# A state space recurrence taken two time steps at a time, inside a two-block transformer kernel

## What is computed

```python
lr, li = f32(lam_re), f32(lam_im)
dt = jnp.exp(f32(log_dt))[:, None]
mag = jnp.exp(lr * dt)
ar, ai = mag * jnp.cos(li * dt), mag * jnp.sin(li * dt)      # lambda
...
bbar_re = kr[..., None] * br - ki[..., None] * bi            # B
bbar_im = kr[..., None] * bi + ki[..., None] * br
def step(carry, uc):                                         # x[t] = lambda x[t-1] + B u[t]
    bur = jnp.einsum('lbgh,gph->lbgp', uc, bbar_re)
    bui = jnp.einsum('lbgh,gph->lbgp', uc, bbar_im)
    _, _, sr, si = lax.associative_scan(_complex_affine_combine, (a_r, a_i, bur, bui), axis=0)
    ...
    y = jnp.einsum('ghp,lbgp->lbgh', cr, xr) - jnp.einsum('ghp,lbgp->lbgh', ci, xi)
y = y + f32(d_skip) * f32(u)
g = jax.nn.gelu(y)
val, gate = jnp.split(g @ w_glu + b_glu, 2, axis=-1)
return val * jax.nn.sigmoid(gate)
```

## Time and profile before

| | us |
|---|---|
| median of 3 runs (lowest, highest) | 2593.39 (2592.49, 2596.54) |
| profiled execution | 2592.58 |
| its span, first to last instruction | 2590.5 |
| PE busy | 2421.6 (93%) |
| DVE busy | 1809.1 (70%) |
| ACT busy | 1261.3 (49%) |
| POOL busy | 159.4 (6%) |
| chain that ended last: PE, DVE, ACT | 84%, 10%, 3% of the span |

### The profile page before, as it was taken

The page is one execution under the profiler, slowest core; times in us unless marked ns, Lnnn a source line. Parts: engine busy times, 40 slices in busy tenths (PEclk is TensorE's granted clock), DMA queues, the critical chain, the costliest instruction groups (busy, mean ns, idle before and its releaser), DMA issues.

```text
span 2590.5 us, 31848 instructions
## 1 busy us (share of the span) xinstructions
PE 2421.6 (93%) x12441; PEld 1937.3 (75%) x12441; DVE 1809.1 (70%) x1966; ACT 1261.3 (49%) x1290; POOL 159.4 (6%) x142
## 2 busy tenths in 40 slices
PE   7999999999999999989989965689999999999996
PEld 6878858788878678789658852367888887887885
DVE  5763348857852477685545459968888888898887
ACT  3432334334322434344334444537667677776674
POOL 0000000000000000000100006500000000000000
PEclk9999999999999999999999985789999999999998
DMA  9767158657756287543245530138999989998994
...
DMA packets 303413, 586.14 MB, mean 226 GB/s; under 512 B 61439, under 2 KB 96965, under 8 KB 303181
## 3 DMA queue, kind: packets, MB, share of 16 engines
...
HBM read 583.60 MB, written 1.06 MB: 226 GB/s over the span
## 4 chain that ended last, share of the span: by engine, by line
PE 84%; DVE 10%; ACT 3%; issue 2%; DMA 1%; DVEq 0%; SPq 0%; ACTq 0%
PE psum L862 19%; PE psum L864 19%; PE psum L863 19%; PE psum L1326 3%; PE psum L895 3%; PE psum L1333 2%; PE psum L1388 2%; PE psum L2049 2%; PE psum L985 2%; DVE ring_r L1062 2%; PE psum L2673 2%; PE psum L2828 1%; PE psum L2851 1%; ACT ring_r L1056 1%; PE psum L1946 1%
## 5 line engine op out<-in xcount | busy, mean ns | idle before, releaser
L1062 DVE TENSOR_TENSOR ring_r<-ring,ring_r 128x2048 fp32r<-128x2048 f32 x286 | 652.6, 2289 | 291.4 <-ACT ring_r L1056 291.0
L1056 ACT CAST ring_r<-ring 128x2048 fp32r<-128x2048 f32 x286 | 545.2, 1910 | 507.3 <-PE psum L864 412.8
L864 PE MATMUL psum<-ring_r,arena_r 128*128 128x512 f32 (+1 forms) x1560 | 596.9, 383 | 0.0
L862 PE MATMUL psum<-ring_r,arena_r 128*128 128x512 f32 (+1 forms) x1016 | 400.3, 394 | 10.1 <-DVE arena_r L2846 5.2
L1062 DVE TENSOR_TENSOR ring_r<-ring,tail_r 128x2048 fp32r<-128x2048 f32 x143 | 327.2, 2288 | 95.9 <-ACT tail_r L1056 95.8
L863 PE MATMUL psum<-ring_r,arena_r 128*128 128x512 f32 (+1 forms) x1016 | 390.6, 384 | 0.0
L1056 ACT CAST tail_r<-ring 128x2048 fp32r<-128x2048 f32 x143 | 273.2, 1910 | 145.3 <-PE psum L864 139.3
L864 PEld LDWEIGHTS psum<-ring_r,arena_r 128*128 128x128 f32 x1560 | 294.4, 189 | 58.4
L864 PE MATMUL psum<-ring_r,z_r 128*128 128x512 f32 (+1 forms) x840 | 310.6, 370 | 0.0
L862 PEld LDWEIGHTS psum<-ring_r,arena_r 128*128 128x128 f32 x1016 | 192.3, 189 | 57.9 <-issue 18.5
L863 PEld LDWEIGHTS psum<-ring_r,arena_r 128*128 128x128 f32 x1016 | 192.3, 189 | 37.7 <-issue 1.9
...
## 6 DMA issues: line engine op xcount, KB each, us to landing
...
```

Of the source, the lines that this page charges most:

```text
L862: pe.matmul(dst, lhs_low, rhs, start=start, stop=False)
L864: return pe.matmul(dst, lhs, rhs_low, start=False, stop=stop)
L1056: act.copy(upper[i % UPPERS], place(PN[r.key, i])).then_inc(upper_ready, 1)
L1062: dve.tensor_tensor(low, raw, upper[i % UPPERS], ALU.subtract).then_inc(lower_ready, 1)
```

## The change

Time is split into 128 pairs of steps. The state is kept only at even steps: x[2m] = lambda^2 x[2m-2] + lambda B u[2m-1] + B u[2m], so B gets a second copy, `b_next` = lambda B, the drive of a pair is the sum of two matmuls, and scans have 128 steps with factor mag^2 (`l_mag2`). The even outputs are C x[2m]; the odd ones are (C lambda) x[2m] + K u[2m+1], where K = C B is a matrix of one block (`same_step` on PE, 32x32 tiles; `copy_kernel` on ACT). C lambda (`CT_next`) is made on POOL. The rotation is needed at 128 steps only. All buffers of the stage halve, so `scanned` has eight places instead of four.

Moved: the scaling of B goes from behind feed-forward 4 into four of its last iterations (pieces 0 to 3, two for B and two for lambda B); the loads of C are issued at the end of feed-forward 4 and not after the last turning of B; the turnings of lambda B lie on PE in units 0 and 2; outputs of block k come in step 2k+4, and the last but one behind the loop; GELU of the first half and the first three weight roundings lie on ACT behind the last placing of C. The skip term of block k is added two blocks later.

```diff
@@ -1162,6 +1180,8 @@
+            if r.n == 4 and "s5" in stages and UP_HALVES + 4 <= i < UP_HALVES + 8:
+                s5_scale_b_dve(dve, step, i - UP_HALVES - 4)
...
@@ -2297,28 +2317,36 @@
+    PAIRS = SEQ // 2
...
+    rot = cv.take(2, 2, QUAD, PAIRS)
+    glu_xh = Carve(cv.at, of=arena_r).take(KD, SEQ)
...
+        act.activation(l_mag2, lam_dt, ACT.Exp, scale=2.0).then_inc(*s5A.inc("mag2"))
...
+        for out_, other, op in ((l_kr2, l_ki, ALU.subtract), (l_ki2, l_kr, ALU.add)):
+            dve.tensor_tensor(l_t1, l_lr, l_kr if out_ is l_kr2 else l_ki, ALU.mult)
+            link(dve.tensor_tensor(l_t2, l_sin, other, ALU.mult))
+            link(dve.tensor_tensor(out_, l_t1, l_t2, op))
...
-        sp.wait_ge(*s5P.after("bt3"))
+        sp.wait_ge(halves_used, 5 * FFN_HALVES)
...
+            if k >= 2 and n % 2 == 0:
-            pool.tensor_tensor(prods[k % 2][:, 0:2, j, :], scanned[:, n % 4, :, :, :], both(r[:, 0, :, :]), ALU.mult)
-            pool.tensor_tensor(prods[k % 2][:, 2:4, j, :], scanned[:, n % 4, :, :, :], both(r[:, 1, :, :]), ALU.mult)\
-                .then_inc(*s5G.inc(f"x{n}"))
+            pool.tensor_tensor(prods[:, k % 2, 0:2, j, :], scanned[:, n % 8], both(r[:, 0]), ALU.mult)
+            pool.tensor_tensor(prods[:, k % 2, 2:4, j, :], scanned[:, n % 8], both(r[:, 1]), ALU.mult).then_inc(*s5G.inc(f"x{n}"))
+            if n % 2 == 0:
+                continue
+            c, after = CT[:, k % 2], CT_next[:, k % 2]
+            pool.wait_ge(*s5A.after(f"ct{k}"))
+            if k >= 1:
+                pool.wait_ge(*s5G.after(f"c{k - 1}"))
+            pool.tensor_tensor(after, c, lam_of(l_lr, k, 3), ALU.mult)
+            pool.tensor_tensor(c_part, c[:, 0:2], lam_of(l_sin, k, 2), ALU.mult).then_inc(*step.one())
+            pool.wait_ge(*step.now())
+            pool.tensor_tensor(after[:, 0], after[:, 0], c_part[:, 1], ALU.add)
+            pool.tensor_tensor(after[:, 1], after[:, 1], c_part[:, 0], ALU.subtract)
+            pool.tensor_tensor(after[:, 2], after[:, 2], c_part[:, 1], ALU.subtract).then_inc(*s5G.inc(f"c{k}"))
...
+        def copy_kernel(k):
+
+            act.wait_ge(*s5P.after(f"kb{k}"))
+            act.copy(kernel_0[:, k % 2, :], bank(7)[:, SEQ:SEQ + P]).then_inc(*s5A.inc(f"kc{k}"))
...
         angles(0)
         rotations(0)
+        copy_b(4)
+        copy_b(5)
         for k in range(KD):
             if k + 1 < KD:
                 angles(k + 1)
             place_c(k)
+            if k >= 1:
+                copy_kernel(k - 1)
             if k + 1 < KD:
                 rotations(k + 1)
+            else:
+                gelu(act, 0)
+            if k == 0:
+                copy_b(6)
+                copy_b(7)
+        copy_kernel(KD - 1)
         act.copy(glu_ones, ones[0:1, :]).then_inc(*s5A.inc("ones"))
         act.wait_ge(bias_landed, 16)
         act.copy(bias_hi, z_row[0:1, :]).then_inc(*s5A.inc("bias"))
-        gelu(act, 0)
         glu_upper_act(act, 0, None)
-        glu_upper_act(act, 1, s5V.after(f"in{S5_UNITS - 1}"))
+        glu_upper_act(act, 1, None)
+        glu_upper_act(act, 2, None)
         gelu(act, 1)
-        glu_upper_act(act, 2, s5P.after("y7"))
-        glu_upper_act(act, 3, None)
...
-                mag = l_mag[:, state:state + 1].to_broadcast([P, SEQ])
+                mag = l_mag2[:, state:state + 1].to_broadcast([P, PAIRS])
                 for i in range(2):
-                    ins = dve.tensor_tensor_scan(scanned[:, n % 4, i, jj, :], mag, bu[:, 1 - i, jj, :], 0.0, ALU.mult, ALU.add)
+                    ins = dve.tensor_tensor_scan(scanned[:, n % 8, i, jj, :], mag, bu[:, 1 - i, jj, :], 0.0, ALU.mult, ALU.add)
             ins.then_inc(*s5V.inc(f"scan{n}"))
-            if n % 2 and k >= 1:
...
+            if k < 2:
+                pe.wait_ge(*s5A.after("bt7"))
+            else:
+                pe.wait_ge(*s5V.after(f"y{k - 2}"))
+            even, odd = (bank(6 - k % 2)[:, i * PAIRS:(i + 1) * PAIRS] for i in range(2))
             for i, v in enumerate((0, 1, 1, 2)):
                 for j in range(QUAD):
-                    own_rows = slice(32 * j, 32 * j + 32)
-                    mm = pe.matmul(bank(6)[own_rows, 0:SEQ], CT[:, k % 2, v, j, :], prods[k % 2][:, i, j, :],
-                                   start=i == 0, stop=i == 3)
+                    pe.matmul(even[channels(j), :], CT[:, k % 2, v, j, :], prods[:, k % 2, i, j, :], start=i == 0, stop=i == 3)
+            pe.wait_ge(*s5A.after(f"kc{k}"))
+            pe.matmul(odd, kernel_0[:, k % 2, :], x_at[:, k, 1, :], start=True, stop=True)
+            pe.wait_ge(*s5G.after(f"c{k}"))
+            for i, v in enumerate((0, 1, 1, 2)):
+                for j in range(QUAD):
+                    mm = pe.matmul(odd[channels(j), :], CT_next[:, k % 2, v, j, :], prods[:, k % 2, i, j, :],
+                                   start=False, stop=True, skip_group_check=True)
             mm.then_inc(*s5P.inc(f"y{k}"))
 
         def turn_c(k):
             if k == 0:
...
+        def same_step(k):
+
+            pe.wait_ge(*s5A.after(f"ct{k}"))
+            if k >= 1:
+                pe.wait_ge(*s5A.after(f"kc{k - 1}"))
+            for part in range(2):
+                for j in range(QUAD):
+                    mm = pe.matmul(bank(7)[channels(j), SEQ + 32 * j:SEQ + 32 * j + 32],
+                                   b_wide[:, part, QUAD * k + j, :, :].rearrange("p g h -> p (g h)"), CT[:, k % 2, part, j, :],
+                                   start=part == 0, stop=part == 1)
+            mm.then_inc(*s5P.inc(f"kb{k}"))
...
+            if n == KD:
+                pe.wait_ge(*s5A.after("bt7"))
+            for i in range(2):
+                for j in range(2):
+                    rows_ = channels(2 * u + j)
+                    pe.matmul(driven(n)[:, i, j, :], BT[rows_, 0, i, k, :], x_at[rows_, k, 0, :], start=True, stop=True)
+                for j in range(2):
+                    rows_ = channels(2 * u + j)
+                    mm = pe.matmul(driven(n)[:, i, j, 1:PAIRS], BT[rows_, 1, i, k, :], x_at[rows_, k, 1, 0:PAIRS - 1],
+                                   start=False, stop=True, skip_group_check=True)
             mm.then_inc(*s5P.inc(f"bu{n}"))
...
+            k, odd = divmod(n, 2)
...
```

231 lines of the change are left out of this document (135 added, 96 removed).

## The result

The changed kernel takes **2547.07 us** (median of 4 runs, 2546.78 to 2547.86) against 2593.02 for the kernel before: a ratio of 0.9819, 95% interval 0.9804 to 0.9833. The forecast was 2550.5, range 2540 to 2566. The profiled execution took 2547.86 us, its span is 2546.0 (before 2590.5), and the mean granted clock of TensorE is 0.971 (before 0.961).

A forecast was written before the change was run, and what follows sets the result against it. It took DVE to bound the state space stage, with a small loop through ACT's sines, and PE the experts. Terms -46.8 - 1.9 + 4.5 - 2.5 + 1.1 + 2.8 = -42.8 gave 2549.8, median 2550.5 us, range 2540 to 2566.

The forecast's parts named there:

- The recurrence: State space stage: halved DVE work plus a gap for ACT's sines, period 8.2 us instead of 14.16, saving 46.8 us.
- PE late for one and a half blocks: State space stage: PE at the low clock is late for the first blocks with outputs, +4.5 us, bounds 0 and +28.
- The sign that I gave: State space stage: PE's granted clock would be 0.5 in the first blocks and 1.0 later.
- rival 1: State space stage: PE is the bound for most of it at a low clock; 2561, up to 2574 us; chance 0.23.
- POOL: State space stage: products halve, C lambda adds 3.0 us; sum 7.9 us a block, only 0.3 below the period.
- The norm: Ahead of the stage: scaling of B moved into earlier DVE idle time lets the norm start sooner, -2.5 us.
- The constants: mLSTM opening: six more small DVE operations, with PE waiting for the DVE step behind them, +1.1 us.
- the table load: mLSTM opening: the exponential's table load on ACT, 1.28 us, expected to cost 0.
- The first unit: Start of the state space stage: first angles and sines half as long, so it starts 1.9 us sooner.
- The tail: Last scan to last skip term: ACT's order delays PE's first GLU product, 12.5 us instead of 9.8, +2.8 us.
- Rival 3: Whole change: all covers hold, PE is never late, the tail keeps its length; 2543 us; chance 0.13.

The follow-up runs named there:

- angle_early: Changed kernel with DVE's angle of the next block moved from behind the odd unit's sums to ahead of its products: 2544.86 us.
- pool_more: Changed kernel with POOL's first C lambda product of each block made twice, with a wait between: 2547.47 us.
- all_three: Changed kernel with the six small constant operations moved into the last FFN, the bias cast behind the third weight cast, and DVE's angle ahead of the odd products: 2542.01 us.
- all_four: all_three with the third plane of C lambda made by ACT instead of POOL, except in the last block: 2540.21 us.
- scale_behind: Changed kernel with the last two of four scaling pieces put back behind DVE's last weight half of the last FFN: 2550.33 us.
- bias_later: Changed kernel with ACT's cast of the GLU bias moved from ahead of the first weight cast to behind the third: 2544.16 us.
- second trace of the changed kernel: The changed kernel run and profiled again with nothing altered: median 2546.53 us.

## Why the prediction was right, point by point

- **The recurrence: right.** 8.08 us a period against 8.2, the last block 6.8 as forecast (1607.13 to 1613.89), a gap of 0.40 that ACT's sines end. Saved 47.9, forecast 46.8 (the forecast's own terms, 7 x 8.2 + 6.8, make 64.2 and not 64.4, so 47.0). A scan of 128 costs 0.34 us (1.35 / 4), I had 0.32; DVE's work is 7.68 us a period (I had 7.6) and the gap 0.40 (0.6; 0.77 in the first two periods), so the loop through ACT is a little shorter than I made it. angle_early shows that the loop is what I took it for: take ACT's sines out of it, and 2.8 us go.
- **PE late for one and a half blocks (+4.5): wrong.** It was never late. The sign that I gave, a clock of 0.5 in the first blocks and 1.0 later, did not come either: behind the first block it went up and down (0.98, 0.66, 0.92, 0.71). The step that failed is the price at the low clock, taken halfway to records: 4.2 us for 64 output records, 2.3 for a unit's inputs, 1.3 for the same-step matrix, where the rows have 3.7, 2.0 and 0.4 (only the product with the same-step matrix was dearer, 0.7 against 0.5). Columns decide: 32 records of 128 columns cost 1.94, where 32 of 256 cost 3.64. And I let a block be at one clock throughout, though the clock comes back within the block that PE is busy in. The Trainium skill, page "TensorEngine Tiling (Array Packing)", Tiling Modes, has the drain at each change of mode, which I had weighed as part of rival 1. The 16 records of a unit's inputs (1586.42 to 1587.60) take 1.18 us in the changed kernel, the 8 of twice the columns 1.14, and 2.08 against 2.08 at the low clock: twice the records cost next to nothing more, and with seven changes a block PE still fits. No run here shows a price of the drain by itself.
- **POOL: right.** C lambda takes 2.7 us a block (I had 3.0), the sum is 7.6 to 7.7 (7.9). pool_more crosses the period and pays 2.8 us, all of it in the tail. On the other side the margin didn't show: with the period at DVE's own 7.7 us, as full as POOL, all_three kept its gain, and relieving POOL (all_four) added none.
- **The norm (-2.5): right**, -2.6, and scale_behind brings it back. The four pieces, at 3.3 us in gaps of 3.15, cost nothing that the rows show.
- **The constants (+1.1): right in its own step, too small in its effect.** The operations cost 1.1 us and the table load nothing. What I left out is that PE, whose wait they lengthen, can come out of a longer wait with a lower clock: 1.5 us more in seven of 14 traces, the first of the changed kernel among them. The 2.2 us at the norm are scatter.
- **The first unit (-1.9): -1.5.** ACT's four copies of the turned B now wait for PE between each other (0.27 us in the rows) and take 2.81 us instead of 2.21.
- **The tail (+2.8): right in mechanism, 0.9 too large.** ACT's chain sets it (bias_later), PE comes in at the low clock. The first product began 3.0 us behind the last scan (I had 4.4), and the last outputs ran at the high clock, 2.5 us instead of 3 to 4.
- **The sum.** I was 1.9 us high in the profiled execution (2549.8 against 2547.86). PE's 4.5 us that didn't come, 1.1 more from the recurrence and 0.9 less tail (6.5) were offset by 3.7 us of clock ahead of the last FFN, 0.9 behind the GLU and 0.4 of the first unit (5.0); the rest are tenths. The range held with all of them, but that the median came within 3.4 us of the number is in part luck: 4.5 us for a PE that wasn't late stood in for 3.7 us of clock in the opening and at the norm, for which I had no term. Rival 3 (2543), whose recurrence is the one that was measured (its tail is not), came within 3 us of the second trace of the changed kernel (2545.6).
